# Moving the last readout and the last copy of a head ahead of the next head's first block, and its recurrent low parts from VectorE to GpSimd

## What is computed

```python
h = _rmsnorm(x, norm_g[l])
xa, ga, q, ckv, gb, qi, ki, wi = jnp.split(jnp.einsum('bsd,de->bse', h, w_in[l]), IN_SPLITS, axis=-1)
ya = _rglru_branch(xa, ...) * jax.nn.silu(ga)
# group B, per head h and block of 128 queries:
logits = (q_abs . c_sel) * HEAD_DIM**-0.5 + rel_bias[bucket]      # selected keys alone
p = jax.nn.softmax(logits, axis=-1)
o = p @ c_sel ;  yb = (o @ w_uv) * jax.nn.silu(gb)
x = x + jnp.einsum('bse,ed->bsd', jnp.concatenate([ya, yb], -1), w_out[l])
```

## Time and profile before

| what | us |
|---|---|
| median of three runs (1632.14 to 1632.33) | 1632.24 |
| the profiled execution, its own time | 1631.82 |
| its span in the profile | 1630.1 |
| granted TensorE clock, mean over the span | 0.995 of full speed |
| PE busy / PE weight loads busy | 1588.7 / 1324.9 |
| DVE / ACT / POOL busy | 854.2 / 580.1 / 431.7 |

### The profile page before, as it was taken

The page is one execution under the profiler, slowest core; times in us unless marked ns, Lnnn a source line. Parts: engine busy times, 40 slices in busy tenths (PEclk is TensorE's granted clock), DMA queues, the critical chain, the costliest instruction groups (busy, mean ns, idle before and its releaser), DMA issues.

```text
span 1630.1 us, 21564 instructions
## 1 busy us (share of the span) xinstructions
PE 1588.7 (97%) x7595; PEld 1324.9 (81%) x7595; DVE 854.2 (52%) x1498; ACT 580.1 (36%) x845; POOL 431.7 (26%) x289
## 2 busy tenths in 40 slices
PE   7999999999999999999999999999998899999998
PEld 7788999888888888888888888777776788888886
DVE  6427555577777877875555555376777100031003
ACT  6325555433444443332111111355555222232321
POOL 2222222222222222222222222110010344444650
PEclk9999999999999999999999999999999999999999
DMA  7212111122212122223222221321222522237322
GB/s 262 83 49 72 46 45 39 33 55 62 61 55 65 33 63 68 68 84 97 77 71 77 71 77 51 110 85 61 71 73 81 217 94 100 94 101 298 132 85 103
DMA packets 132312, 141.38 MB, mean 87 GB/s; under 512 B 8519, under 2 KB 103849, under 8 KB 129961
## 3 DMA queue, kind: packets, MB, share of 16 engines
q1 hardware_dynamic: 130728, 136.55, 26.2%
q0 software_dynamic: 1536, 4.20, 0.8%
HBM read 116.08 MB, written 24.64 MB: 86 GB/s over the span
## 4 chain that ended last, share of the span: by engine, by line
PE 83%; issue 8%; DVE 4%; ACT 2%; POOL 1%; DMA 1%; DVEq 0%; SPq 0%; ACTq 0%; POOLq 0%
PE ps L1039 17%; PE ps L1040 17%; PE ps L1041 17%; PE ps L1315 6%; PE ps L1317 6%; PE ps L1316 6%; PE ps L1142 2%; PE ps L1144 2%; PE ps L1256 2%; PE ps L1220 2%; PE ps L1233 1%; PE ps L1342 1%; PE ps L1341 1%; PE ps L1340 1%; PE ps L1240 1%
## 5 line engine op out<-in xcount | busy, mean ns | idle before, releaser
L1039 PE MATMUL ps<-hT_hi,w_lo 128*128 128x512 f32 (+1 forms) x1344 | 511.9, 381 | 3.2 <-POOL w_lo L663 3.2
L1040 PE MATMUL ps<-hT_lo,w_hi 128*128 128x512 f32 (+1 forms) x1344 | 509.9, 379 | 0.0
L1041 PE MATMUL ps<-hT_hi,w_hi 128*128 128x512 f32 (+1 forms) x1344 | 509.8, 379 | 0.0
L663 POOL TENSOR_TENSOR w_lo<-w_raw,w_hi 128x512 fp32r<-128x512 f32 x168 | 240.7, 1436 | 758.4 <-ACT w_hi L743 758.4
L1039 PEld LDWEIGHTS ps<-hT_hi,w_lo 128*128 128x128 f32 x1344 | 252.6, 188 | 48.6 <-issue 5.4
L1040 PEld LDWEIGHTS ps<-hT_lo,w_hi 128*128 128x128 f32 x1344 | 252.7, 188 | 43.4 <-issue 0.2
L1041 PEld LDWEIGHTS ps<-hT_hi,w_hi 128*128 128x128 f32 x1344 | 252.7, 188 | 42.7
L743 ACT ACTIVATE w_hi<-w_raw 128x512 fp32r<-128x512 f32 x168 | 104.8, 629 | 479.0 <-PE ps L1041 472.7
L1315 PE MATMUL ps<-wo_hi,hT_lo 128*128 128x512 f32 x448 | 175.2, 391 | 3.1 <-DVE hT_lo L1584 3.1
L1643 DVE TENSOR_TENSOR res<-ps,res 128x512 f32<-128x512 f32 x32 | 21.8, 691 | 295.7 <-PE ps L1317 245.0
L1316 PE MATMUL ps<-wo_lo,hT_hi 128*128 128x512 f32 x448 | 174.8, 390 | 0.0
(11 more groups left out here) (190 smaller groups left out, 1825.8 us busy)
## 6 DMA issues: line engine op xcount, KB each, us to landing
w_raw<-in_w_in SPq DMA_DIRECT2D x168, 256.0 KB, 2.8
wo_raw<-in_w_out SPq DMA_DIRECT2D x64, 512.0 KB, 3.6
xin<-in_x SPq DMA_DIRECT2D x8, 1024.0 KB, 6.0
res<-in_x SPq DMA_DIRECT2D x8, 1024.0 KB, 10.6
out<-res SPq DMA_DIRECT2D x16, 512.0 KB, 5.0
y_lru_dram<-sg SPq DMA_DIRECT2D x8, 512.0 KB, 2.8
q_dram<-av SPq DMA_DIRECT2D x8, 512.0 KB, 3.8
gate_dram<-rg SPq DMA_DIRECT2D x8, 512.0 KB, 4.3
```

Source lines behind the costliest of these rows:

```text
L663: nc.gpsimd.tensor_tensor(w_lo[:, j, :, :], w_raw[:, j, :, :], w_hi[:, j, :, :].bitcast(F32), ALU.subtract).then_inc(w_lo_s, 1)
L1039: nc.tensor.matmul(o, wlo, hi, start=(kt == 0), stop=False)
L1040: nc.tensor.matmul(o, whi, lo, start=False, stop=False)
L1041: return nc.tensor.matmul(o, whi, hi, start=False, stop=(kt == KT - 1))
```

## The change

Three edits, all in the attention stage.

1. PE: `turn_p(h+1, 0)` goes behind `read_out(h, 3)`.
2. ACT: `softexp(h+1, 0)` goes behind `p_copy(h, 7)`; both first exponentials of the next head follow it.
3. `low_y` goes from DVE to POOL: `low_y(h, 0)` behind the second gate load of a head, `low_y(h, 1)` behind the fourth, ahead of `low_wk`. It waits for ACT's high part there as before.

```diff
@@ POOL
+            def low_y(h, k):
+
+                pool.wait_ge(yl_hi, 2 * h + k + 1)
+                piece = (slice(None), ds(h, 1), slice(k * NT, (k + 1) * NT))
+                nc.gpsimd.tensor_tensor(hT_lo[piece], yl_raw[:, :].rearrange("p (o s) -> p o s", o=1),
+                                        hT_hi[piece].bitcast(F32), ALU.subtract).then_inc(yl_lo, 1)
+
             def gate_loads(h):
                 for r in range(4):
                     pool.wait_ge(o_used, 4 * h + r + 3)
                     pool.dma_start(gate[:, r % 2, :], gate_d[ds(h, 1), :, 2 * r * P:2 * (r + 1) * P].rearrange(
                         "o p s -> (o p) s")).then_inc(gate_ld[r % 2], 16)
+                    if r % 2 == 1:
+                        low_y(h, r // 2)
@@ ACT
                     p_copy(h, q)
-                    if q + 2 >= QB and not last:
-                        softexp(h + 1, q + 2 - QB)
+                    if q + 1 == QB and not last:
+                        softexp(h + 1, 0)
+                        softexp(h + 1, 1)
@@ PE
                         logits(h + 1, 2, 1 - p, turn_next)
                         logits(h + 1, 3, 1 - p, turn_next)
-                        turn_p(h + 1, 0)
...
                 read_out(h, 3, p, last)
+                if not last:
+                    turn_p(h + 1, 0)
@@ DVE
-                    if q in (2, 5):
-                        low_y(h, q // 5)
```

More of the change, by code:

```diff
@@ L1585, in cut_y @@
                    ).then_inc(y_att, 1)
[L1587 to L1592, removed]
             def dve_head(h, p, turn, last=False):
```

## The result

| | before | after |
|---|---|---|
| median, us | 1632.19 (1631.25 to 1632.33, 4 runs) | 1621.27 (1621.2 to 1621.4, 4 runs) |
| profiled execution, its own time / span, us | 1631.82 / 1630.1 | 1621.2 / 1619.5 |
| mean granted TensorE clock | 0.995 | 0.995 |

The ratio is 0.9933, with a 95% interval of 0.9919 to 0.9947. The kernel became 10.9 us faster. The prediction was 1623.1 us, a gain of 9.1, with a range of 1621.7 to 1627.0. The measured time lies 0.4 us under its low end, so the range missed it.

What follows compares the result with a forecast made beforehand. PE, busy 97% of the span, was taken as the bound, its reachable holes being waits at head turns. Six turns (8.6 us) plus turn 6 to 7 and the end (0.5) gave 9.1 us: median 1623.1, range 1621.7 to 1627.0.

Steps and rivals of the forecast that it cites:

- The mechanism: At each head turn, PE's 1.17 us wait before the transpose goes; PE and ACT edits belong together; a head takes 26.8 us.
- Rival D: At the turn on PE, `read_out` still waits for `p_copy(h,7)`, 0.5 us late: median 1625, chance 0.06.
- The term of the turn: Turns out of heads 0 to 5: 1.53 us won on PE less 0.1, net 1.43 each, 8.6 in six.
- the dead heat at `gated(h,3)`: Second half of part 0: PE may go on at 1189.15 and asks at 1189.12; 0.1 us a turn charged.
- Who waits on DVE: At the turn, `cut_y(h,1)`'s copy and subtraction wait for POOL's `low_y` and `low_wk`; DVE comes 0.45 to 0.65 us later.
- rival A: At the turn, DVE's copy beats POOL and PE waits nowhere: 9.9 us gained, median 1622.3, chance 0.22.
- Turn 6 to 7 and the end: `gated(6,3)` comes earlier and the last copy and POOL's subtractions shift along: 0.5 us gained, bounds 0.7 and -1.5.
- B: PE's wait moves to `gated(h,3)`, DVE 1.1 us later still: 2 us gained, median 1630 (half the delay 1626.5), chance 0.14.
- C: `low_y` on POOL takes 3.13 us each turn, DVE 2.35 us late; slower from 1.9 us delay: median 1638, chance 0.04.

## Why the prediction was right, and where it was wrong

**The mechanism** was right. PE and ACT belong together: apart they give nothing (1632.41, 1631.2), together 10 us. The idle time of the transposes fell to 3.7 us (3.5 foretold), `p_copy(h,7)` came 0.28 us before `read_out` (0.2), `low_y` took 1.29 us (1.3). A head is 26.6 us, where 26.8 was forecast and 27.3 would have refuted it. Rival D didn't happen.

**The term of the turn** failed by its size: 1.43 us forecast, 1.62 measured, and six of them make 1.1 of the 1.8 us that the forecast missed. It has two parts. First, I took 0.11 us off for the transpose, because it still has to be done behind `read_out`. It costs 0.02 there: the rows show 0.02 us between its start and that of `kv_mm`, and from `read_out` to `kv_mm` it is 3.27 us where it was 3.26 without a transpose between them. The price came from eight transposes in a row, and one between two long flows of matmuls costs less. So even my upper bound of 1.53 a turn was too low, and the low end of the range, which was worked out from it, was too high. Second, I put 0.1 us for the dead heat at `gated(h,3)`. There was none, since the copy won and DVE came 0.46 us earlier instead of 0.5 later: that is the step below.

**Who waits on DVE.** This step failed. I took the copy as the loser at the turn, since it had lost in six heads of six. It won in all six, as rival A had it, and lost in head 6, as I had it (1.66 us measured, 1.6 foretold). The rule of the Trainium skill, SBUF — State Buffer, Who interferes with whom, gives the pair to the instruction that issues first. In heads 0 to 5 of the changed kernel the rows agree: the copy, recorded first, was through in 0.31 us. In the kernel before (1.13 or 1.14 us), in the run with `low_wk` first (2.36) and in heads 6 and 7 of the changed kernel (1.66 and 1.67) they don't, as far as recorded starts show issue. My reason for rival A, one more waiting instruction on POOL, fell with its own run.

The 0.46 us that DVE won by it are worth nothing: with `low_y` left on DVE the copy lost to `low_wk` alone (1.13 us), DVE kept its old timing, and the heads were 26.6 us long as well. But the case that I forecast is another one, a copy and a subtraction that lose to both POOL operations, with `softmin(h+1,0)` 0.45 to 0.65 us later than before. The run with `low_wk` first shows that lateness: 2.83 us from the copy's start (1176.62) to `softmin(h+1,0)` (1179.45) instead of 2.20, 0.63 later. It cost 0.37 us a head, 2.2 us in six, not the 0.1 us a turn that I put for it. At that price the changed kernel would have taken some 1623.5 us, an estimate from 1621.27 + 6 x 0.37. So the winner decided some 2 us. That the forecast of 1623.1 lies near this estimate is luck: the transpose was priced too high, and the lateness too low.

**Turn 6 to 7 and the end:** 0.5 us forecast, 0.69 - 0.22 = 0.47 measured. The last copy took 1.78 us (1.76 before) and PE waited 3.08 (3.07), so this part shifted along as I said.

**Outside the turns:** 0.26 us ahead of the first turn and 0.18 in the output projection I had at nothing, 0.44 together. No run was made for them, but both are of the size by which executions differ there anyway: nine of the profiled ones took 357.79 to 358.05 us in an output projection that no edit touches, and the starts of head 0 differ by 1.5 us. The last 0.3 of the 1.8 us is the step from the profiled execution to the median. I added the 0.4 us of the kernel before; in the changed kernel it was 0.07.

**Rivals B and C** are real couplings, only not at this size. B's wait on `gated(h,3)` is what the run with `low_wk` first shows, at 0.37 us a head. When POOL's queue at the turn is 2.4 or 3.5 us longer, the kernel goes to 1628.38 and 1634.47. I put C's threshold at 1.9 us of delay against DVE's timing before the change, and that was about right. By the line of the table a turn's 1.62 us are gone when DVE comes 0.7 + 1.62 = 2.3 us later than in the changed kernel. There DVE is 0.46 us earlier than before, so this is 1.9 us against the timing before.

**The range** was built on my own bounds of the terms and had 0.6 us below rival A's 1622.3. An upper bound that takes a saving from rows at full flow must also allow that the moved instruction costs nothing: 0.11 x 6 = 0.7 us would have taken the low end to 1621.0, and held the time. Rival A with the transpose at its true price gives about 1621.8, so the last half microsecond would still have been held by the width of the range and not by its reasons.

## What to carry to other kernels

When two engines each have a waiting instruction ahead of work that is ready, look for both before moving one: moved alone, the edit on PE only gave the wait another name, and the one on ACT left it as it was. Before a contention is priced, ask how much slack its victim has at the place where it meets the critical engine; here 0.7 us made a loss of up to 0.7 us free and every further microsecond full price. And look at the granted clock behind each longer wait of PE: in both kernels compared here a wait of 3.08 us cost 1.5 us more than its own length.

## What the runs showed of the hardware that was not expected

- A two-input subtraction of DVE that meets a row of POOL operations may be passed over by all of them: 4.37 us behind 2.37 + 1.28 + 0.73. This happened in 8 of 30 turns of five kernels, in some turns of an execution and not in others. Otherwise it got in behind the first.
- The recorded starts don't tell which of a DVE copy and a POOL subtraction waits: with POOL 0.22 to 0.24 us behind, the copy took 0.31 us ahead of the loop's `low_y`, 1.14 ahead of `low_wk`, and 1.66 ahead of `low_y` in head 6.
- The granted clock went down to 0.50, the 1.2 GHz level, for 3 us behind PE's wait of 3.08 us in the profiled executions before and after the change. It did so, to 0.50 to 0.75, in nine of ten executions with this wait. Behind the wait of 2.23 or 2.24 us in head 7 it was low in seven of twelve (0.57 over 4 us in the run with the PE and ACT orders alone) and 1.00 in the other five, the changed kernel among them. There the matmul group took up to 1.6 us more, but the head only 0.6 to 0.9, since later waits take up part of it.
